# Expert values: a dense weight matrix over a streamed table in place of a gather per slot

## The reference, cut to what matters

```python
q  = (h2 @ w_query)                      # 8 heads x 2 halves x 128
s1, s2 = q[.., 0] @ keys[0], q[.., 1] @ keys[1]      # 128 scores per side
v1, i1 = top_k(s1, 16);  v2, i2 = top_k(s2, 16)
best, sel = top_k(v1[:, None] + v2[None, :], 16)     # of the 256 sums
idx  = (i1 * 128 + i2)[sel]              # 16 of 16384 experts per head
gate = softmax(best)
act  = gelu(h2 . u_tab[idx])             # 128 slots per token
y    = sum over slots of gate * act * v_tab[idx]
x    = x + gate2 * rms(y)
```

## Time and profile before

| what | us |
|---|---|
| median of 3 runs | 3824.27 (3820.43 to 3825.89) |
| span of the profiled execution | 4199.6 |
| first gather of the expert stage, from the span's start | 904.62 |
| DVE busy in the span | 2313.6 (55%) |
| POOL busy | 2152.0 (51%) |
| PE busy | 3314.8 (79%) |
| DMA moved in the span | 1245.51 MB, mean 297 GB/s |

### The profile page before, as it was taken

One profiled execution on the slowest core, in us unless ns is written; L12 is line 12 of the kernel. 1 busy time (PEld: TensorE's weight loads), 2 busy tenths in 40 slices (PEclk: granted clock), 3 DMA queues, 4 the chain that ended last, 5 costly groups with the idle time before them and its releaser, 6 DMA issues.

```text
span 4199.6 us, 38180 instructions
## 1 busy us (share of the span) xinstructions
PE 3314.8 (79%) x9348; PEld 1593.5 (38%) x9348; DVE 2313.6 (55%) x5821; ACT 950.0 (23%) x2161; POOL 2152.0 (51%) x2222
## 2 busy tenths in 40 slices
PE   8998989928777777877777777777777777887677
PEld 2454555513333333333333333333333333333222
DVE  2104552867755665555665655566555665556442
ACT  1003773312221221112112211211121121112111
POOL 0000300236566665666666666566666665666665
PEclk9999999969898898898888888888888888888888
DMA  9104102159999999999999999899999999999997
GB/s 357 64 15 126 32 19 113 61 188 352 344 357 359 353 359 354 347 368 343 341 359 347 350 356 344 332 354 355 360 347 358 358 357 348 343 363 358 361 362 303
DMA packets 365168, 1245.51 MB, mean 297 GB/s; under 512 B 52129, under 2 KB 57505, under 8 KB 362751
## 3 DMA queue, kind: packets, MB, share of 16 engines
q0 software_dynamic: 313504, 1141.02, 72.4%
q1 hardware_dynamic: 48852, 96.77, 6.6%
q10 hardware_dynamic: 2576, 5.10, 0.4%
HBM read 1220.34 MB, written 22.39 MB: 296 GB/s over the span
## 4 chain that ended last, share of the span: by engine, by line
PE 38%; issue 17%; another core or an unknown queue 9%; DVE 5%; DMA 4%; POOL 3%; ACT 1%; DVEq 0%; POOLq 0%; ACTq 0%; SPq 0%
PE ps_y L1692 33%; PE ps_q L950 5%; DMA urow<-in_u_tab,idx 3%; POOL urow L1473 2%; POOL vrow L1473 1%; DMA vrow<-in_v_tab,idx 1%; DVE urow L1612 1%; ACT diag L1580 1%; DVE aux L993 0%; PE ps_s L961 0%; DVE i L996 0%; DVE sel L996 0%; DVE i L992 0%; DVE aux L1029 0%
## 5 line engine op out<-in xcount | busy, mean ns | idle before, releaser
L1692 PE MATMUL ps_y<-vrow,diag 128*128 128x512 f32 (+1 forms) x4352 | 2220.8, 665 | 647.5 <-issue 329.9
L1612 DVE CUSTOM_DVE_ANT_0 urow<-urow,ps_h 128x1024 f32<-128x1024 f32 x1088 | 1299.8, 1220 | 1025.2 <-DMA urow<-in_u_tab,idx 865.6
L1692 PEld LDWEIGHTS ps_y<-vrow,diag 128*128 128x128 f32 (+1 forms) x4352 | 884.3, 209 | 1893.6 <-issue 1576.9
L1473 POOL DMA_INDIRECT vrow<-in_v_tab,idx x1088 | 1031.6, 948 | 785.7 <-issue 287.4
L1473 POOL DMA_INDIRECT urow<-in_u_tab,idx x1088 | 1030.7, 947 | 430.5 <-issue 282.8
L1580 ACT ACTIVATE diag<-const,wgt 128x128 f32<-128x128 f32 x1024 | 373.1, 396 | 1766.2 <-PE ps_y L1692 643.3
L950 PE MATMUL ps_q<-aux,w_q_sb 128*128 128x128 f32 x2048 | 271.7, 292 | 58.1 <-issue 49.4
L950 PEld LDWEIGHTS ps_q<-aux,w_q_sb 128*128 128x128 f32 x2048 | 263.9, 207 | 94.4 <-issue 93.2
L1293 POOL TENSOR_TENSOR xo<-xo,ot 128x1024 f32<-128x1024 f32 (+1 forms) x9 | 21.1, 2343 | 352.2 <-DVE ot L1249 352.2
L530 PE MATMUL ps_z<-hT,w_in_sb 128*128 128x512 f32 (+1 forms) x576 | 190.5, 491 | 4.6 <-DVE hT L448 4.6
L625 POOL MEMSET kTs<- 128x384 f32 x1 | 0.4, 418 | 322.7 <-POOLq L344 322.7
(11 more groups left out here) (181 smaller groups left out, 2341.3 us busy)
## 6 DMA issues: line engine op xcount, KB each, us to landing
ada<-in_w_ada SPq DMA_DIRECT2D x12, 2048.0 KB, 12.5
urow<-in_u_tab,idx POOLq DMA_INDIRECT x1088
vrow<-in_v_tab,idx POOLq DMA_INDIRECT x1088
w_in_sb<-in_w_in SPq DMA_DIRECT2D x8, 1024.0 KB, 17.9
w_q_sb<-in_w_query SPq DMA_DIRECT2D x8, 1024.0 KB, 14.3
x<-in_x_p ACTq DMA_DIRECT2D x8, 512.0 KB, 6.6
w_out_sb<-in_w_out SPq DMA_DIRECT2D x8, 512.0 KB, 7.0
xo<-in_x_p SPq DMA_DIRECT2D x8, 512.0 KB, 3.7
```

The lines of the kernel that those rows point to most:

```text
L1473: nc.gpsimd.indirect_dma_start(ring[k % RING][:, :], None, A[table][:, :], bass.IndirectOffsetOnAxis(ap=places[:, col:col + 1], axis=0)).t ...
L1612: nc.vector.tensor_tensor_reduce(out=urow[k % RING][:, :], in0=urow[k % RING][:, :], in1=ps_h[:, :], scale=1.0, scalar=0.0, op0=ALU.mult, ...
L1692: last = nc.tensor.matmul(ps_y[0:rows, c], diag[s % DIAGS][:, 0:rows], vrow[k % RING][:, c], start=(s == 0), stop=(s == PH * width(n) - 1))
```

## The change

The queries of all tiles come first inside experts(): PE computes 24 steps (3 groups of up to 512 tokens x 8 heads), ACT copies the scores out, SP stores them to s_d in memory, and ACT loads them back a unit (one tile, one head) at a time. While this runs, the first units are already gathered and multiplied. DVE runs `search(u + 2)` behind `products(u)`, for 72 units, the sample last. output() no longer searches and takes the sample tile last.

The u side stays as it was, with a ring of 7. The v side is new for the prompt tokens. Per pair of tiles (256 tokens) a dense matrix of 16384 x 256 weights is built in the first 32 slots of the next pair (build_step()). For each token one product of two one-hot matrices over its 128 slots, p1 (second index) and p2 (first index, times weight), gives the token's 128 x 128 weights. Four tokens are a group; 64 groups a pair; two groups a step. DVE makes p1 of both groups and p2 of the even one, POOL p2 of the odd one, PE multiplies, ACT copies out. Then PE multiplies the dense matrix with v_tab, which SP streams in 128 chunks of 128 rows through a ring of 3, for all four products of a chunk. For the last pair the build lies in the sample's units. The sample's own v rows are still gathered, 64 of them, and added up by DVE at the end.

Cut from the diff, in this order: constants, output(), build_step(), SP's chunk(), POOL's gather(), hot() and loop, PE's groups and stream, ACT's dense_out(), DVE's hot() and loop:

```diff
-RING = 8
-DIAGS = 4
+URING = 7
+VRING = 3
+LA = 2
...
-    tiles = TILES[-1:] + TILES[:-1]
+    tiles = TILES
...
+BUILD_STEPS = 32
+def build_step(u, k):
+    m = u // (2 * PH) - 1
+    if m < 0:
+        return None
+    j = slots(u) + k - slots(2 * PH * (m + 1))
+    return (m, j) if j < BUILD_STEPS else None
...
+            def chunk(j):
+                if j >= VRING:
+                    sp.wait_ge(v_used, j - VRING + 1)
+                sp.dma_start(vring[j % VRING][:, :], v_v[j % NCH]).then_inc(v_full[j % VRING], 16)
...
+            def gather(table, q, places):
+                if q >= URING:
+                    pool.wait_ge(u_used, q - URING + 1)
+                nc.gpsimd.indirect_dma_start(uring[q % URING][:, :], None, A[table][:, :],
...
+            def hot(m, j):
+                g = m * GROUPS + 2 * j + 1
+                if j == 0:
+                    pool.wait_ge(it_read, 2 * (m + 1))
+                if g >= 2:
+                    pool.wait_ge(b_done, g - 1)
+                for t in range(4):
+                    col = 4 * (g - m * GROUPS) + t
+                    last = nc.gpsimd.tensor_scalar(p2[g % 2][:, t, :], iota, iT[:, 0, col:col + 1],
+                                                   wT[:, col:col + 1], ALU.is_equal, ALU.mult)
+                last.then_inc(hot_pool, 1)
...
+            for u in range(UNITS):
+                for k in range(width(u)):
...
+                    gather("u_tab", slots(u) + k, places)
+                    if build_step(u, k):
+                        hot(*build_step(u, k))
...
+                for j in range(GROUPS):
+                    g = m * GROUPS + j
+                    pe.wait_ge(hot_dve, g + 1)
+                    if j % 2:
+                        pe.wait_ge(hot_pool, g // 2 + 1)
+                    if j >= 2:
+                        pe.wait_ge(b_read, g - 1)
+                    for t in range(4):
+                        last = nc.tensor.matmul(ps_b[g % 2][:, t * P:(t + 1) * P], p1[g % 2][:, t, :], p2[g % 2][:, t, :],
+                                                start=True, stop=True, skip_group_check=True)
+                    last.then_inc(b_done, 1)
...
+                for c in range(NCH):
+                    j = m * NCH + c
+                    pe.wait_ge(v_full[j % VRING], chunk_full(j))
+                    for t in range(2):
+                        for half in range(2):
+                            last = nc.tensor.matmul(ps_y[t][:, 512 * half:512 * (half + 1)], dense[c // 64][:, c % 64, t * P:(t + 1) * P],
+                                                    vring[j % VRING][:, 512 * half:512 * (half + 1)],
+                                                    start=(c == 0), stop=(c == NCH - 1))
+                    last.then_inc(v_used, 1)
...
+                for half in range(2):
+                    src = ps_b[g % 2][:, :].rearrange("p (t c) -> p c t", t=4)[:, 64 * half:64 * (half + 1), :]
+                    last = nc.scalar.activation(dense[half][:, :, 4 * j:4 * j + 4], src, ACT.Copy)
+                last.then_inc(b_read, 1)
...
+            def hot(m, j):
+                for jj in (2 * j, 2 * j + 1):
+                    g = m * GROUPS + jj
+                    if jj == 0:
+                        dve.wait_ge(it_read, 2 * (m + 1))
+                    if g >= 2:
+                        dve.wait_ge(b_done, g - 1)
+                    last = nc.vector.tensor_tensor(p1[g % 2][:, :, :], iota[:, None, :].broadcast_to([P, 4, P]),
+                                                   iT[:, 1, 4 * jj:4 * jj + 4, None].broadcast_to([P, 4, P]),
+                                                   ALU.is_equal)
+                    if jj % 2 == 0:
+                        for t in range(4):
+                            col = 4 * jj + t
+                            last = nc.vector.tensor_scalar(p2[g % 2][:, t, :], iota, iT[:, 0, col:col + 1],
+                                                           wT[:, col:col + 1], ALU.is_equal, ALU.mult)
+                    last.then_inc(hot_dve, 1)
...
+            search(0)
+            search(1)
+            for u in range(UNITS):
+                products(u)
+                if u + LA < UNITS:
+                    search(u + LA)
+                weights(u)
```

More of the change, by code:

```diff
@@ new lines, in experts @@
+        h2T = carve(KC * TOK, k=KC, t=TOK)
+        qs = [carve(2 * 512, s=2, t=512) for _ in range(2)]
+        ss = [carve(512, t=2, c=256) for _ in range(2)]
+        rows = [carve(D) for _ in range(2)]
+        keys = carve(2 * PH * NKEY, a=2 * PH, b=NKEY)
+        assert at <= 64 * 256, at
+        uring = [sb(f"urow{i}", [P, D]) for i in range(URING)]
+        vring = [sb(f"vrow{i}", [P, D]) for i in range(VRING)]
+        s_t = [sb(f"s_t{i}", [P, 2, NKEY]) for i in range(3)]
+        h2n = sb("h2n", [P, D])
@@ new lines, in _ @@
+            for t in range(4):
+                rows_load(t)
+                if t == 1:
+                    sp.dma_start(keys[:, :, :], A["keysT"][:, :, :]).then_inc(keys_in, 16)
+            for g in range(3):
+                for h in range(PH):
+                    i = g * PH + h
+                    if i >= 1:
+                        store(i - 1)
+                    if g < 2 and h < len(qgroups[g + 1][2]):
+                        rows_load(qgroups[g + 1][2][h])
+            store(NH - 1)
@@ L1468, in _ @@
+            for m in range(PAIRS):
+                for c in range(NCH):
+                    if c == VRING and m > 0:
+                        finish(m - 1)
+                    chunk(m * NCH + c)
+            finish(PAIRS - 1)
+            sp.wait_ge(y_out, 16 * NT)
         @block.gpsimd
         def _(pool):
-            def gather(table, ring, full, n, h, k):
-                col = width(n) * h + k
-                places = idx0 if is_sample(n) else idx
-                nc.gpsimd.indirect_dma_start(
-                    ring[k % RING][:, :], None, A[table][:, :],
-                    bass.IndirectOffsetOnAxis(ap=places[:, col:col + 1], axis=0)).then_inc(full[k % RING], 16)
@@ new lines, in _ @@
+            h2_load(0)
+            for t in range(4):
+                h2T_out(t)
+            copy_h2(0)
+            nu = 0
+            for i, (g, h) in enumerate(hsteps):
+                queries_out(i)
+                if i:
+                    scores_out(i - 1)
+                if g < 2 and h >= 4:
+                    for t in qgroups[g + 1][2][h - 4:h - 3]:
+                        h2T_out(t)
+                if 1 <= i <= 3:
+                    s_load(i - 1)
+                    if i >= 2:
+                        exp_gate(i - 2)
+                if i >= 4 and i % 2 == 0:
+                    s_load(nu + 3)
+                    unit(nu)
+                    nu += 1
@@ new lines, in products @@
+            def products(u):
+                if u % PH == 0:
+                    dve.wait_ge(h2_copied, 2 * (u // PH + 1))
+                if u >= 2:
+                    dve.wait_ge(gelu_done, u - 1)
+                for k in range(width(u)):
+                    q = slots(u) + k
+                    row = uring[q % URING]
+                    dve.wait_ge(u_full[q % URING], filled(q))
+                    nc.vector.tensor_tensor_reduce(out=row[:, :], in0=row[:, :], in1=ps_h[:, :], scale=1.0, scalar=0.0,
+                                                   op0=ALU.mult, op1=ALU.add,
+                                                   accum_out=dots[u % 2][:, k:k + 1]).then_inc(u_used, 1)
+                    if build_step(u, k):
+                        m, j = build_step(u, k)
+                        hot(m, j)
+                        if m and j in FIN_DVE:
+                            finish(2 * m - 2 + FIN_DVE[j])
@@ L1638, in finish @@
-                nc.vector.tensor_tensor(y[r, :], y[r, :], x1[r, :], ALU.add).then_inc(y_done, 1)
-            FINISH = 5
-            AHEAD = 2
-            PER = PH * find.PASS + FINISH
-            def start():
-                products(0, 0)
-                weights(0, 0)
-                dve.wait_ge(g2_in, 48)
-                for i in range(2):
-                    own.link(nc.vector.tensor_tensor(g2[i][:, :], g2[i][:, :], gpost[:, :], ALU.mult))
-                assert own.n == AHEAD, own.n
```

897 lines of the change are left out of this document (451 added, 446 removed).

## The result

The changed kernel takes 4397.68 us in the median of four runs (4387.85 to 4405.7), beside 3822.57 (3820.43 to 3825.89) of before: a ratio of 1.1502, with a 95% interval of 1.1485 to 1.152. It is slower, as forecast, but by 575 us where 234 were forecast, and above the range. The profiled execution is the quickest of the four: 4387.85 us with a span of 4386.1. Each of the four has its span on record, 1.75 to 1.85 us under its own time, so the 12 us between this span and the median are those 2 and the spread of the runs. Before's profiled span was 375 us over its median.

A forecast was written before the change was run, and what follows sets the result against it. It took the kernel before as gather-bound, its DMA engines full. 825 + 88 + 490 + 2094 + 207 + 465 = 4169 us profiled, less 111 gives 4058, slower by 6% than 3824; range 3830 to 4340.

The forecast's parts named there:

- the circle: In the build, POOL's next gather waits behind its scalings, these for PE, PE for DVE: 11.3 us in two steps.
- the bounds of the stretches: DVE sets the normal units, DMA the units beside the stream with PE close behind, PE alone the last 440 us.
- the build step: One of 32 steps per pair building the dense matrix: 5.65 us, bounds 3.6 and 7; two units with it 206.
- the 111 us given back: Three stretches beside the stream, 37 us less each in an unprofiled run: 4169 us profiled becomes 4058.
- First product, queries and sixteen units: Start of the kernel: output stage ends at 825 us, 88 to the first product, 490 for sixteen units.
- beside-the-stream stretches: 14 units beside the value stream after each of three builds, bound by DMA: 492 us profiled, or 452 at 408 GB/s.
- the end: Last stream with nothing long beside it, 440 us, and 25 for the two norms after it: 465.
- Build at DVE's pace: Ring stays deep, a build step costs 3.6 us: 3796 us; with port conflict 4.2 and 3872; chance 0.14.
- Starved stream: Stream chunks queue behind seven gathers, about 5 us a chunk rather than 3.44: 4613 us; chance 0.10.
- Bytes decide: Whole kernel: only DMA counts, 247 MB fewer at 391 GB/s give 3190 us; chance 0.03.
- No early start: Queries do not run beside the first units, 24 query steps come first: about 4260 us; chance 0.05.
- The scalings lock too: In the build, DVE's four scalings also shut POOL out, about 1 us in each of 128 steps: 4186; chance 0.13.

The follow-up runs named there:

- the written-out kernel: The kernel before with its hardware loop over the tiles written out, nothing else: 3802.78 us, ratio 0.9955.
- The run with the lead and the split: The changed kernel with each u gather issued five slots ahead of POOL's one-hot step, and two of POOL's four scalings moved to DVE: 3976.75 us, ratio 1.0403.

## Why the prediction was wrong

The direction, the circle and the bounds of the stretches were right. Two terms failed: the build step, in its links of PE and POOL, and the 111 us given back at the end.

**The order of stages.** First product, queries and sixteen units: the first build starts at 1420.9 us, where the sum has 825 + 88 + 490 = 1403. The first product comes at 944.8 instead of 913, the units take 476 instead of 490. Together 18 us late. Part of the 32 at the start is visible on PE, whose first transposes wait for the keys until 848.32. The beside-the-stream stretches were taken as 492 and came at 487.7, 487.6 and 491.8 (9 us less in all); the end as 465, came at 474.4.

**The build step failed.** "That is 11.3 us in two steps: 5.65 us each" was the right circle with two wrong prices. By its own links, forecast against the chain of the trace:

| link of a turn of two steps | forecast, us | measured, us |
|---|---|---|
| PE | 1.7 | 3.80 |
| POOL's four scalings | 1.8 | 3.83 |
| gather, issue and landing | 4.24 | 4.37 |
| DVE, product and one-hots | 3.6 | 2.87 |
| gaps | 0 | 0.32 |
| sum | 11.3 | 15.2 |

For PE I priced one group of eight records. POOL's wait needs the odd group, which stands behind the even one on PE: sixteen records stand in the circle, and at the clock level of this stretch (0.56 granted) they take 3.80 us. For POOL I took 0.45 from the 2.93 us of a 1024-column row, little more than the eighth part; that row also has one per-partition operand where the build's scaling has two. The 128-column scaling takes 0.78 at least and 0.90 on the mean. A duration taken in proportion to size has hardly a fixed part, and for DVE, where I had two sizes to draw a line through, the forecast of 0.25 was close (four take 1.04 in the chain). DVE's link is shorter than forecast, since PE starts on the even group before DVE's second comparison. The gather was right: 3.35 us from the end of the 1.02 us issue to the landing, for the 3.0 taken. The Trainium skill, DMA: Bandwidth & Descriptors, section on the SWDGE path, gives an estimate of 3.2 for this size by its fit; the trace agrees within 0.15 us, counted from the end of the issue.

The three builds beside units and the sample's came to 254.0 + 253.4 + 254.0 + 262.3 = 1024 us, where the sum had 3 x 206 + 207 = 825: 199 us. A step of 7.6 us instead of 5.65 alone makes 62 us a build. Some 15 of them come back, since what lies beside the steps took 10 us, for the 25 of searches, refill and finish() in the sum; without that luck the miss would be larger. With 18, -9 and 9 of the stages above, that is the whole 217 between the forecast span of 4169 and 4386.1.

**The 111 us given back failed.** "In an unprofiled run the gather-bound stretches shrink" took it for granted that what slowed the gathers in the one profiled execution of before comes with profiling, so that the profiled execution of after would have it and its runs would not. No other profiled execution shows such a thing: that of the changed kernel and those of all its variants and the written-out kernel lie among their own kernel's runs, 2 us under their time, and the 21 later executions of before span 3814.4 to 3826.0. The changed kernel's beside-the-stream stretches move 388 GB/s, so there was nothing to give back. Its median lies 12 us above its profiled span. 217 + 111 + 12 = 340 is all of the miss. What slowed that one execution of before stays open.

**The rivals.** *Build at DVE's pace* priced a step at 3.6 to 4.2 us and the kernel at 3796 to 3872, with 3.8 us as the point of change. The run with the lead and the split reached DVE's pace, 4.0 us in its first build, and took 3976.75, some 130 us more than the forecast's sum gives for such a step: DVE's pace exists, but its time was wrong, mostly by the 111 us, and the point of change is 3.2 us by the runs, under the 3.5 of DVE's own half. With its build as written, the scheme could by this estimate not pass before, however its waits are ordered. *Starved stream*: chunks landed in 6.8 us on the page, through three buffers, and the stretches stayed at 488, so no. *Bytes decide*: nearly excluded, and rightly; DMA is idle for most of four builds. *No early start*: the first product comes at 944.8 with query steps still on PE, so no. *The scalings lock too*: the rows of DVE and POOL in one turn of the build say who pays, and for what (timeline, columns as in the earlier trace rows).

```profile
1500.48 0.69 DVE L1723 TENSOR_TENSOR hot<-const,iT 128x512 f32<-128x512 f32 x1
1501.08 1.18 DVE L1729 TENSOR_SCALAR hot<-const,iT,wT 128x128 f32<-128x128 f32 x4
1501.18 3.83 POOL L1358 TENSOR_SCALAR hot<-const,iT,wT 128x128 f32<-128x128 f32 x4 [5.01 <-PE ps_dense L1458]
1502.11 0.68 DVE L1723 TENSOR_TENSOR hot<-const,iT 128x512 f32<-128x512 f32 x1
1507.27 3.13 POOL L1358 TENSOR_SCALAR hot<-const,iT,wT 128x128 f32<-128x128 f32 x4 [1.06 <-PE ps_dense L1458]
```

With DVE idle POOL's four take 3.13 us, beside DVE's comparisons and scalings 3.83, and up to 4.24 in other turns; DVE's own keep their length but for some of its scalings (0.42 us for one of four, 0.34 otherwise). Over the kernel POOL pays (0.895 - 0.78) x 512 = 59 us of its time, where the rival had 128. In the earlier trace rows DVE was the loser, here it is POOL. The Trainium skill, SBUF — State Buffer, section on the two separate sides, lets the loser of the shared ports block for a whole instruction; the trace agrees in size, since the loss follows the time spent beside the comparisons, DVE's two-operand instructions. The trace of the changed kernel also separates the two kinds. POOL's scalings beside the u product alone take 0.78 to 0.79 us, as with DVE idle. The 135 that meet one-hot work of DVE grow, by a fit over all of them (an estimate), by 0.78 us for each us beside a comparison and by 0.05 for each us beside DVE's scalings. So the scalings did not lock, and the rival is out.

**What the whole change does.** It takes away 246 MB, about 600 us at the 409 GB/s of the written-out kernel before. It gives them back in the builds, where DMA moves 68 GB/s, in the first units, which DVE holds to 303, and in the last stream, with PE alone at 153. Without one-hot work the sum is a gain of 3.6%; with it, in the written order, a loss of 15%. Another remedy, a build of the next pair spread over the stream of the last, was not tried: it needs a second dense matrix of 16 MB in SBUF.

## What to carry to other kernels

When an engine both issues transfers and computes under a wait, follow its instruction order once around: a wait placed between two transfers can put the whole circle of engines between them, and moving the transfer one slot ahead of the wait (a few lines on one engine) was worth 251 us of 4398 here. In such a circle count every group that stands ahead of the released one, and price small instructions on an engine from two sizes or not at all. A fall in bytes pays only where the engines can keep DMA full; ask, for each stretch of the new kernel, what else is now the longest.

Where the span of the one profiled execution differs from the median of the runs, run the same kernel again, and look at the spans of those runs before the difference is used in a sum. A variant of the kernel whose span and median agree proves nothing by itself: here the unchanged kernel's did too, when it was run again.

## What the hardware showed unexpectedly

- POOL's scaling with two per-partition operands took 0.78 us for 128 columns; one with a single such operand took 2.93 for 1024. If the second operand costs nothing, about 0.47 us on the line through these do not depend on size (an estimate). DVE's took 0.26 each back to back (four in 1.04).
- One execution of the kernel before spanned 4199.6 us, where 21 others spanned 3814.4 to 3826.0. Its gathers ran at some 350 GB/s where the written-out kernel has 409, in its written-out tiles as in its loop. The cause is open.
- POOL's scalings lost 0.78 us for each us beside DVE's two-operand comparisons and next to nothing (0.05) beside DVE's scalings, by a fit over one trace.
- The same kernel on the same bytes was 0.45% faster (18 us) with the loop written out.
- One core moved 409 GB/s in most slices of the expert stage, with gathers alone or with gathers and plain chunks.
- Where PE worked 112 of 240 us in short groups, its clock was granted at 0.56, between the levels of 1.2 and 2.4 GHz but near the lower. With three more products of 512 columns in each step it was 0.84 (1440 to 1500 us), and eight records of 128 columns right behind them took 1.0 to 1.25 us instead of 2.05; sixteen records that came after 3.38 us of idle time still took 3.0.
